# Hybrid encoder block on eight cores: key and query stores tracked by tile, u and v ahead of gates, one bias product per bank, transpositions by block of use

## The reference, cut to what matters

```python
n = rms_norm(h, g_mix); proj = n @ w_in                 # 1024 -> 7168
q, k, v, z, g = split(proj)                             # 1024 1024 1024 2048 2048
q, k = rope on the first 16 of 64 dims of each head map
a = diff_attention(q, k, v, lam)                        # 8 heads, 2 maps of 64, chunk-causal (64)
a = rms_norm(a, g_subln) * (1 - lam_init)
u, v2 = split(gelu(z)); v2 = layer_norm(v2, ln_g, ln_b)
sgo = u * (W_s-masked @ v2 + b_s)                       # per window of 128, 8 groups of 128 channels
g_a, g_s = split(sigmoid(g))
h = h + (g_a * (a @ w_branch_attn) + g_s * (sgo @ w_branch_sg)) @ w_out
h = h + cross_attention(rms_norm(h), rms_norm(mem), ...)   # 256 memory tokens, 4 heads
h = h + square(relu(rms_norm(h) @ w_ff1)) @ w_ff2
return rms_norm(h, g_final)
```

## Time and profile before

| | us |
|---|---|
| median of 3 runs (5362.1 to 5918.04) | 5904.96 |
| the profiled execution | 5311.49 |
| its span, slowest core | 5309.9 |
| TensorE busy | 4515.7 |
| ScalarE busy | 2630.4 |
| VectorE busy | 2009.2 |

### The profile page before, as it was taken

One profiled execution on the slowest core, in us unless ns is written; L12 is line 12 of the kernel. 1 busy time (PEld: TensorE's weight loads), 2 busy tenths in 40 slices (PEclk: granted clock), 3 DMA queues, 4 the chain that ended last, 5 costly groups with the idle time before them and its releaser, 6 DMA issues.

```text
span 5309.9 us, 97237 instructions; the slowest of 8 cores (5290.9 to 5309.9 us)
## 1 busy us (share of the span) xinstructions
PE 4515.7 (85%) x35128; PEld 2367.8 (45%) x35128; DVE 2009.2 (38%) x3534; ACT 2630.4 (50%) x3744; POOL 261.7 (5%) x343
## 2 busy tenths in 40 slices
PE   4282849489878989999899999999999999998988
PEld 2031424244444645445554554455455455554433
DVE  3272534243443324324423332432343253234253
ACT  2031525355555746555655665565565567554211
POOL 0000000001011100000000000100000000000000
PEclk8596979799999989999999999999999999999989
DMA  9837374747665543354245345333543533442533
GB/s 238 151 111 150 114 145 130 144 133 173 169 159 146 148 141 110 103 174 126 88 134 161 108 120 165 112 101 125 159 118 115 168 114 103 138 153 92 184 119 111
DMA packets 520569, 724.34 MB, mean 136 GB/s; under 512 B 23017, under 2 KB 384873, under 8 KB 517482
## 3 DMA queue, kind: packets, MB, share of 16 engines
q1 hardware_dynamic: 508986, 678.27, 42.3%
q0 software_dynamic: 11120, 39.85, 6.2%
HBM read 671.23 MB, written 126.48 MB: 150 GB/s over the span
## 4 chain that ended last, share of the span: by engine, by line
PE 68%; DMA 11%; DVE 8%; issue 5%; ACT 4%; SPq 3%; DVEq 0%; another core or an unknown queue 0%; POOL 0%; ACTq 0%; POOLq 0%
PE ps L360 67%; DMA Qd<-mergedT 6%; ACT PT L367 4%; SPq L357 3%; DMA nTd<-G 1%; DVE sm L569 1%; DVE nb L381 1%; PE ps L364 1%; DVE sm L568 1%; DVE o L370 1%; DVE h L370 1%; DVE T L370 1%; DMA Kt<-U 1%; DVE t L370 1%; DMA Kc<-Kt 1%
## 5 line engine op out<-in xcount | busy, mean ns | idle before, releaser
L367 ACT ACTIVATE PT<-ps 128x1024 bf16<-128x1024 f32 (+3 forms) x2304 | 2058.7, 953 | 1152.9 <-PE ps L360 1150.6
L360 PE MATMUL ps<-Vc,PT 128*128 128x129 bf16 x16896 | 1204.4, 224 | 24.3 <-POOL PT L370 7.6
L360 PEld LDWEIGHTS ps<-Vc,PT 128*128 128x128 bf16 x16896 | 989.6, 99 | 462.1 <-issue 452.2
L360 PE MATMUL ps<-QTh,Kc 64*128 64x512 bf16 (+3 forms) x4608 | 709.6, 373 | 292.7 <-DMA Kc<-Kt 197.2
L360 PE MATMUL ps<-wp,G 128*128 128x512 bf16 x3072 | 727.9, 390 | 212.7 <-DVE G L385 201.0
L360 PE MATMUL ps<-nT,wp 128*128 128x512 bf16 (+1 forms) x3712 | 831.1, 378 | 18.5 <-DMA nT<-nTd 14.3
L360 PEld LDWEIGHTS ps<-wp,G 128*128 128x128 bf16 x3072 | 296.7, 100 | 550.1 <-issue 250.6
L360 PEld LDWEIGHTS ps<-nT,wp 128*128 128x128 bf16 x3712 | 356.2, 98 | 405.1 <-issue 33.1
L360 PEld LDWEIGHTS ps<-QTh,Kc 64*128 64x128 bf16 x4608 | 157.4, 94 | 741.7 <-issue 717.7
L360 PE MATMUL ps<-G,wp 128*128 128x512 bf16 x1536 | 370.1, 389 | 80.2 <-DVE T L370 38.8
L370 POOL TENSOR_TENSOR PT<-PT,mask_s 128x256 bf16<-128x256 bf16 x320 | 249.4, 791 | 3578.1 <-ACT PT L367 3576.8
(11 more groups left out here) (99 smaller groups left out, 2791.6 us busy)
## 6 DMA issues: line engine op xcount, KB each, us to landing
wp<-wb_ff SPq DMA_DIRECT2D x128, 1024.0 KB, 5.7
wp<-wb_in SPq DMA_DIRECT2D x106, 1024.0 KB, 7.6
Vc<-Vs SPq DMA_DIRECT2D x288, 258.0 KB, 3.2
Kc<-Kt SPq DMA_DIRECT2D x288, 256.0 KB, 3.6
h<-xp SPq DMA_DIRECT2D x96, 512.0 KB, 5.9
Vs<-SV SPq DMA_DIRECT2D x16, 1032.0 KB, 9.6
wb_ff<-w_ff POOLq DMA_DIRECT2D x8, 2048.0 KB, 22.5
wp<-wb_ba SPq DMA_DIRECT2D x16, 1024.0 KB, 5.4
```

The source lines that it names most:

```text
L360: P.op("pe", lambda e: e.matmul(out, lhsT, rhs, start=start, stop=stop, skip_group_check=True), reads=rd, writes=wr)
L367: P.op("act", lambda e: e.activation(out=out, in_=in_, func=func, **kw), reads=rd, writes=wr)
```

## The change

- **Stores.** Kt and Qd of a stage are tracked by eight buffers in place of two, one for each transfer. Each store reads only its own column group's buffers of t, and copies and rotations write only theirs.
- **Order of weights.** The casts and panels of u and v come ahead of those of gates.
- **Start.** The first table load comes at hook 7 (was 12), ahead of leave for the third panel (hook 8, was 7). The five replicated vectors are loaded at the start of `xprep_pre` instead of hook 36.
- **Solo part.** u, v, then gates. The first scalar_tensor_tensor of the layer norm follows each v block's statistics; `ln_root` and the four `ln_apply` stand after the sixth gate group. The three "gap" rounds go.
- **Spatial mixing.** One bias product of 512 columns opens a bank, then four products with WsT.
- **Blocks.** After the output product, each block is transposed and goes through the first score panel at once; the transpositions Tp(2), Tp(3) stand in the first panel of the next product; the first panel of ff1 is done by block too, in 32 matmuls of 128 columns a block. `softnorm` comes a round later. Three more "gap" rounds go.

```diff
-                        b_o = b_Kt[g][half]
+                        b_o = b_Kt[g][half * 4 + c]
...
-                    dma("sp", o, t[:, c, :], b_t, [b_o], f"{kind}st{half}")
+                    n = len(b_t) // 4
+                    dma("sp", o, t[:, c, :], b_t[n * c:n * (c + 1)], [b_o], f"{kind}st{half}")
...
-                    copy(dst(c), ps[:, bk, :], [b_ps[bk]], b_t)
+                    copy(dst(c), ps[:, bk, :], [b_ps[bk]], bd(c))
...
         def xprep_pre():
+            vectors()
...
+                        stt(h[:, b, :], h[:, b, :], MVt[:, 2 * b:2 * b + 1], vrep[4][:], ALU.subtract, ALU.mult,
+                            [b_h[b], b_mv[b], b_vrep[4]], [b_h[b]])
...
+                    act(gatesT[:, ct, :], ps[:, bk, :], AF.Sigmoid, [b_ps[bk]], [b_G[ct]])
+                    if cg == 1 and ctl == 1:
+                        ln_root()
+                        for b in range(4):
+                            ln_apply(b)
...
+                    mm(ps[:, bk, :], ones1[:], bs2[:, hf * 512:(hf + 1) * 512], True, False, [b_ones1, b_bs2],
+                       [b_ps[bk]])
                     for gl in range(4):
                         gi = hf * 4 + gl
...
-                        mm(o, ones1[:], bs2[:, gi * 128:(gi + 1) * 128], False, True, [b_ones1, b_bs2], [b_ps[bk]])
+                        mm(ps[:, bk, gl * 128:(gl + 1) * 128], nb[n_][:, gi * 128:(gi + 1) * 128], WsT[:, gi, :],
+                           False, gl == 3, [b_nb[n_], b_WsT], [b_ps[bk]])
...
+            s = take(pan(wM, "M", 0, 0))
+            for b in range(4):
+                Tn(b)
+                yield "item"
+                score_unit(s, b, 0)
+                yield "item"
+            free_panel()
...
+            s = take(pan(wb_ff1, "ff10", 0, 0))
+            for b in range(4):
+                Tn(b)
                 yield "item"
...
+                bk = bbank()
+                for ctl in range(4):
+                    for kc in range(8):
+                        mm(ps[:, bk, ctl * 128:(ctl + 1) * 128], wp[s][:, kc, ctl * 128:(ctl + 1) * 128], nT[:, b, kc, :],
+                           ctl == 0 and kc == 0, ctl == 3 and kc == 7, [b_wp[s], b_nT[b]], [b_ps[bk]])
...
-        b_Kt = [bufs(f"Kt{g}_", 2) for g in range(NG)]
+        b_Kt = [bufs(f"Kt{g}_", 8) for g in range(NG)]
...
-        hooks = {4: rotary, 7: lambda: allow(3), 10: lambda: allow(6), 12: lambda: table_load(0),
-                 20: small, 24: lam_prep, 36: vectors}
+        hooks = {4: rotary, 7: lambda: table_load(0), 8: lambda: allow(3), 10: lambda: allow(6),
+                 20: small, 24: lam_prep}
```

More of the change, by code:

```diff
@@ L404, in build_program @@
                       ("xq", w_xq, wb_xq, 0, D, 0, D), ("xo", w_xo, wb_xo, 0, D, 0, D)]
-        for cb_ in (5, 6, 3, 4):
+        for cb_ in (3, 4, 5, 6):
             cast_list.append((f"inb{cb_}", w_in, wb_in, 0, D, cb_ * 1024, (cb_ + 1) * 1024))
@@ L621, in rope_tile @@
                 tt(v3(T[3]), pv_, cv, ALU.mult, [b_ps[bk], b_cos], [b_T[3]])
[L622 to L623 removed]
+                tt(dst(0), T[0][:], T[2][:], ALU.subtract, [b_T[0], b_T[2]], b_dst(0))
+                tt(dst(1), T[3][:], T[1][:], ALU.add, [b_T[3], b_T[1]], b_dst(1))
         def p1_pre(g):
@@ L833, in feat, with ln_root, ln_apply @@
                              lambda kc: [b_wp[s]] + b_src(kc))
-            yield "solo"
[L836 to L843, removed]
+            lnn = {}
+            def ln_root():
+                act(LNRt, MVt.rearrange("p (b two) -> p two b", two=2)[:, 1, :], AF.Ln, b_mv + [b_cf], [b_lnr],
+                    scale=1.0, bias=EPS5)
+                act(LNRt, LNRt, AF.Exp, [b_lnr], [b_lnr], scale=-0.5)
+            def ln_apply(b):
+                n_ = nxt("nb", NNB)
+                stt(nb[n_][:], h[:, b, :], LNRt[:, b:b + 1], vrep[5][:], ALU.mult, ALU.add,
+                    [b_h[b], b_lnr, b_vrep[5]], [b_nb[n_]])
+                lnn[b] = n_
+            yield "solo"
             for cg in range(2):
@@ L864, in post_body @@
             yield "endsolo"
[L865 to L885, removed]
             for b in range(4):
@@ L922, in resid, with tok_unit, Tn @@
                    [b_ps[bk], b_h[b]], [b_h[b]])
[L924 to L953, removed]
+            def tok_unit(s, b, cg, lhs, rd, row):
+                bk = group(lambda kc: lhs(b, kc), lambda kc: wp[s][:, kc, :], lambda kc: [b_wp[s]] + rd(b, kc))
+                resid(bk, b, cg)
+                if cg == 1:
+                    ch[b] = norm_chain(h[:, b, :], [b_h[b]], row, False)
+            def Tn(b):
+                force(ch[b])
+                n_ = ch[b]["n"]
+                transpose8(nb[n_], [b_nb[n_]], nT[:, b, :, :].rearrange("p k t -> p (k t)"), [b_nT[b]])
             def softmax(b, cg, bk):
@@ L970, in Tp, with score_unit, relu_square @@
                 transpose8(Ph[:, b, :], b_U[2 * b:2 * b + 2], AX_[:, b * 1024:(b + 1) * 1024], b_A[2 * b:2 * b + 2])
+            def score_unit(s, b, cg):
+                bk = group(lambda kc: nT[:, b, kc, :], lambda kc: wp[s][:, kc, :], lambda kc: [b_wp[s], b_nT[b]])
+                softmax(b, cg, bk)
+                if cg == 1:
+                    later(1, lambda: softnorm(b))
+            def relu_square(bk, dst, b_dst, view):
+                t_ = nxt("t", 4)
+                act(T[t_][:], ps[:, bk, :], AF.Relu, [b_ps[bk]], [b_T[t_]])
+                tt(dst, view(T[t_]), view(T[t_]), ALU.mult, [b_T[t_]], b_dst)
@@ L972, in post_body @@
+            ch = {}
             for cg in range(2):
-                s = sc[0] if cg == 0 else take(pan(wM, "M", 0, 1))
+                s = take(pan(wb_out, "out", 0, cg))
                 for b in range(4):
[L975 to L978, removed]
+                    tok_unit(s, b, cg, lambda b, kc: mergedT[:, kc, b * 128:(b + 1) * 128], lambda b, kc: [b_mT[kc]], 1)
@@ L979, in post_body @@
                     yield "item"
-                    if cg == 1 and b >= 2:
-                        Tp(b - 2)
+                free_panel()
+            s = take(pan(wM, "M", 0, 0))
[3 more added lines that the diff above has]
+                score_unit(s, b, 0)
+                yield "item"
+            free_panel()
+            s = take(pan(wM, "M", 0, 1))
+            for b in range(4):
+                score_unit(s, b, 1)
+                yield "item"
+                if b >= 2:
+                    Tp(b - 2)
+                    yield "item"
@@ L982, in post_body @@
+            free_panel()
+            ch = {}
+            for cg in range(2):
+                s = take(pan(wVW, "VW", 0, cg))
+                for b in range(4):
+                    tok_unit(s, b, cg, lambda b, kc: PTx[:, b, kc, :], lambda b, kc: b_A[2 * b:2 * b + 2], 2)
+                    yield "item"
+                    if cg == 0 and b < 2:
+                        Tp(b + 2)
                         yield "item"
                 free_panel()
-            yield "gap"
-            for b in (2, 3):
-                Tp(b)
+            s = take(pan(wb_ff1, "ff10", 0, 0))
@@ L992, in post_body @@
+            free_panel()
             for half in range(2):
-                for cgl in range(4):
+                for cgl in range(1 - half, 4):
                     cg = half * 4 + cgl
@@ L1018, in post_body @@
                     free_panel(2)
-        b_Kt = [bufs(f"Kt{g}_", 2) for g in range(NG)]
+        b_Kt = [bufs(f"Kt{g}_", 8) for g in range(NG)]
         b_Vs = [bufs(f"Vs{g}_", 2) for g in range(NG)]
-        b_Qd = [bufs(f"Qd{g}_", 2) for g in range(NG)]
+        b_Qd = [bufs(f"Qd{g}_", 8) for g in range(NG)]
         b_nTd = bufs("nTd", NG)
```

30 lines of the change are left out of this document (16 added, 14 removed).

## The result

| | before | after |
|---|---|---|
| profiled execution, us | 5311.49 | 5123.49 |
| its span | 5309.9 | 5121.9 |
| median of all runs, us | 5633.53 (4 runs) | 5123.56 (4 runs) |
| ratio of like runs | | 0.9587, 95% interval 0.95 to 0.9674 |

Changed by 4.1%: faster. The two profiled executions lie 188 us apart, 3.5%. The forecast was 5104 us, 20 too low.

The account below looks back on a forecast made before the run. Bound by TensorE's own work beside attention and, in projections, 329 us of holes from serial stores and casts. Terms summed to -207 from 5311.49, giving 5104 us; range 4965 to 5225, likeliest case alone 5040 to 5165.

Parts of the forecast that it names:

- The holes: Four projection-stage stretches with TensorE idle, 329 us: stores by tile leave about 50 us a hole, -97 us after give-back.
- 0.376 us each with casts beside them: Packet price from the 33.13 us store over 88 packets; for 96 packets a hole, strict turns would be 0.515.
- casts are the hole: Rival, projection stages: stores, QTh and Kc don't get through before casts end; holes give 30, 5171 us; chance 0.17.
- Strict turns: Alternative queue price in the holes: 0.427 + 0.088 = 0.515 us a packet; four holes would give some 45 us less.
- Stage 0: TensorE's 24.43 us wait until 133.23, for VectorE behind the gsub load: -16; table load before allow(3): +6.
- Vectors: Five vector loads (2.6 MB) leave stage 0 and come ahead of the memory tokens, lengthening a 13.02 us wait: +9.
- Copies into G in 1064 to 1862: TensorE's 47.3 us of waits there, behind an nTd store that follows the query stores: 0 to 47, taken as -20.
- Bias product: Spatial banks beside attention: a step with a bank goes from 2.72 to 2.1 us, 56 banks, -34 (bounds -23, -38).
- Layer norm and gaps: Later stages: layer norm moved under gate groups, extra table loads at 0; removed gaps, 42 x 0.6 over both edits, -25.
- Blocks: Later stages beside attention: fewer VectorE waits in the norm chain -10, ff1 by block +6, plus gap rounds at 0.6 each.
- the rival with 0.158 a matmul: Rival, ff1 by block: 1024 matmuls don't hide weight loads, +106 us more, 5207 to 5265 with its 0.217 case; chance 0.05.
- Last stage: Last stage alone: wait and spatial part -16, transpositions -5, before ff1 -4, softmax blocks -2; sum -27.

## Why the prediction was right or wrong

The total came out 20 us off by luck: errors of both signs met. The mechanism of the stores held, and four terms were mis-sized: the holes by 34 us, the layer norm by 39, the last stage by 21 and the bias product by 13. It took the profiled execution as its base, and by that its 3.9% stands beside 3.5 to 4.1% measured. Set against the median that was shown (5904.96), 5104 us reads as 13.6%, more than three times what happened.

- **The holes**: mechanism right, size wrong. Forecast 50 us a hole and -97; measured 261 us in all, and -63 against the same waits. The first two holes, 81.2 and 78.1 us, lie above the 75 that was to show the step wrong. The failed step is "0.376 us each with casts beside them". The count was right: 96 packets per engine are there. But 0.376 is 33.13 us over 88 packets, and that is a mean over two kinds, as the trace of before shows: 84 per engine passed in the first 11 us (1351 packets, 414.09 to 425), mostly ahead of the casts, and the last 9 took 22 us, in turns with the casts. In the changed kernel the sine and cosine tables, which the count left out, stand in the queue ahead of the 96. From 384.02 on, 6 us go by free of casts, then 20 us in four turns with packets of 32 KB, and the 96 and 8 more take the 43.6 us to 453.64, 0.42 each: 69.6 us, where the prediction had 33 to 46. QTh and Kc then took 6.4, not 11; in the first hole, beside the large packets, Kc alone 21.9. The rival "casts are the hole" gave -30, the forecast -97, and the truth lies between.
- **Strict turns or 0.376**: the turns are strict, 1498 packets against 1497. They are not 0.515 us long, since 0.427 is a mean over packets of 2 KB (0.29 us) and 32 KB (4.6 us). And the sum for them was off: 57 in place of 50 us a hole is 28 us in four holes, not 45.
- **Stage 0**: the wait for the rope's VectorE work went from 24.43 to 11.80 (forecast -16), the wait ahead of it from 16.12 to 21.54 us, +5.4 (forecast +6; 15.37 with the stores alone). Both about right, though about half of the 12.6 came with the other edits of the start.
- **Vectors**: the wait at the memory tokens rose from 13.02 to 22.67 us, +9.7 (forecast +9). What their absence gave the first hole was not in the sum: it is 81.2 us with the move and 94.3 in the kernel with the stores alone.
- **Copies into G in 1064 to 1862**: 47.3 before, 11.4 after by the waits over 3 us, and a new one for Kc of 5.4: -30 (forecast -20).
- **Bias product**: -20.6, forecast -34; the term is the step with a bank, 2.28 us on average in the changed kernel, some 2.4 with this edit alone, and not 2.1.
- **Layer norm and gaps**: the worst step. The prediction priced three gap rounds at 0.6 us each, 13 us beside attention; measured -51.5. The price looked at one round's arithmetic, TensorE against ScalarE. It left out the waits on VectorE around these rounds (nb 9.6, nT 11.8, SV 10.0 us in the stretch before) and the clock: 160 us at 1.2 GHz before, 92 with the edit. Both were in the trace of before.
- **Blocks**: forecast some -12 for their gap rounds, -10 for waits, +6 for ff1; measured nothing beside attention (3046.0 without the edit, 3045.1 with it). "A removed gap is TensorE idleness removed" failed: it is that only where VectorE is ready. The matmuls of ff1 themselves were priced right: 32 take 1.8 to 1.95 us, so the rival with 0.158 a matmul falls, and by this trace a stream of 128-column matmuls with a new weight each is nearer to 0.058 than to the 81 ns of the Trainium skill (TensorE: Matmul & The Clock Gate, section Back-to-back issue gap).
- **Last stage**: forecast -27, measured -6. Banks and the layer norm's wait gave about 14, as thought. The -11 for transpositions failed: the first block's copy now stands on VectorE behind the statistics of the fourth, and TensorE waits 8 us twice. Writing it earlier helped there and cost more elsewhere; the stretch beside attention then grew by 20 us. There TensorE's waits for VectorE's residual sums (h) are 22.8 + 28.4 us, against 9.7 + 8.4, and those for nT fall from 32.4 to 4.8; why the sum grew is open.
- **Hidden at nothing**: table loads rose from 29 to 45 as counted, with no wait of TensorE behind them. "The last y store is gone by then" was wrong (36.9 us of ScalarE), but five banks hid it.

## What to carry to other kernels

A transfer queue that is freed of its waits sends everything at once: size the wait that is left by all that is then queued, packet by packet, each with one packet of the other queue beside it, and ask how large that one is. A mean over packets that ran alone and packets that took turns prices neither. Look whether the other traffic (here casts that leave in a bunch) can be spread, which here was worth as much as the edit itself. Price a removed gap by the whole stretch around it, the clock after it included, and look who used the gap. Say a forecast as a ratio as well as a time, with its base.

## What the runs showed of the hardware

Two DMA queues took strict turns, packet by packet: 1498 and 1497 packets in 35 us, 62 and 64 in the 20 us before them, and 48 and 47 from 425 to 440 us in the kernel before. So what a queue got through beside a cast hung on the size of the cast's packets: 0.37 us a turn at 2 KB, about 4.7 at 32 KB. Sending can block without any wait: with the engines at 100% SP took 36.64 us to send four stores of 128 KB that waited for no semaphore, where such a store is else sent in some 0.5 to 0.8 us; in the kernel before one took 49.77 us, at 937.51. And short waits on TensorE between short matmuls (0.62 and 1.03 us, among the spatial banks) were followed by a fall of the granted clock to 1.2 GHz for most of the next 8 us, with TensorE busy for 18.41 of the 20 us ahead of it.
